# Expert gates spread in three passes over 40, 40 and 48 sub-tiles instead of four passes over 32

## What is computed

```python
q = (h @ wq).reshape(B, S, PEER_HEADS, 2, PEER_HALF)
sc = jnp.einsum('bshcd,cnd->bshcn', q, keys)
# top 16 of each half, then top 16 of the 256 sums, per token and head
expert = i1 * N_SUBKEYS + i2               # 128 * 128 experts
gate = jax.nn.softmax(best_v, axis=-1)
u = jnp.take(u_tab, ex, axis=0)
act = gelu(jnp.einsum('thkd,td->thk', u, hx)) * gx
vv = jnp.take(v_tab, ex, axis=0)
out = jnp.einsum('thk,thkd->td', act, vv)
```

## Time and profile before

| | |
|---|---|
| median of three runs | 2258.52 us |
| the profiled execution's time | 2252.36 us |
| its span | 2250.6 us |
| mean granted TensorE clock | 0.987 of full |
| TensorE matmuls | busy 2162.7 us, 21816 matmuls |
| VectorE | busy 1588.3 us |
| ScalarE | busy 1092.5 us |
| GpSimd | busy 336.4 us |

### The profile page before, as it was taken

One profiled execution on the slowest core, in us unless ns is written; L12 is line 12 of the kernel. 1 busy time (PEld: TensorE's weight loads), 2 busy tenths in 40 slices (PEclk: granted clock), 3 DMA queues, 4 the chain that ended last, 5 costly groups with the idle time before them and its releaser, 6 DMA issues.

```text
span 2250.6 us, 55219 instructions
## 1 busy us (share of the span) xinstructions
PE 2162.7 (96%) x21816; PEld 1939.7 (86%) x21816; DVE 1588.3 (71%) x3080; ACT 1092.5 (49%) x1881; POOL 336.4 (15%) x166
## 2 busy tenths in 40 slices
PE   8889999999999999999998899999999999999997
PEld 8878999988888888788788789999888888887885
DVE  6645896876666667975576458968766666679755
ACT  5534455444444444444454344554444444444443
POOL 0022696000000000000000237950000000000000
PEclk9999999999999999999999999999999999999999
DMA  6212344434444444445342134443344444444451
GB/s 255 94 41 102 143 171 174 142 131 168 167 164 165 164 165 165 149 168 187 134 149 93 41 125 142 181 167 135 131 168 168 168 168 168 166 153 150 167 200 70
DMA packets 46618, 335.04 MB, mean 149 GB/s; under 512 B 5168, under 2 KB 5296, under 8 KB 6320
## 3 DMA queue, kind: packets, MB, share of 16 engines
q1 hardware_dynamic: 46512, 333.61, 41.2%
HBM read 332.54 MB, written 1.05 MB: 148 GB/s over the span
## 4 chain that ended last, share of the span: by engine, by line
PE 80%; issue 6%; POOL 6%; DVE 5%; ACT 1%; DMA 1%; POOLq 0%; SPq 0%; DVEq 0%; ACTq 0%
PE PS L1647 32%; PE PS L1624 23%; PE PS L1309 8%; PE PS L1636 6%; POOL low L435 5%; PE PS L1325 3%; PE PS L1489 1%; DVE low L1083 1%; PE PS L1527 1%; PE PS L1538 1%; DVE hot L1153 1%; DVE hot L1149 1%; DMA ring<-in_w_slabs 1%; ACT high L459 0%; PE PS L1357 0%
## 5 line engine op out<-in xcount | busy, mean ns | idle before, releaser
L648 ACT CAST high<-ring 128x1024 fp32r<-128x1024 f32 x512 | 535.6, 1048 | 602.1 <-PE PS L1624 443.2
L1624 PE MATMUL PS<-hTh,high 128*128 128x256 f32 x2048 | 594.8, 290 | 13.0 <-ACT GA L652 11.0
L1624 PE MATMUL PS<-hTh,low 128*128 128x256 f32 x2048 | 578.4, 282 | 0.0
L1624 PE MATMUL PS<-hTl,high 128*128 128x256 f32 x2048 | 577.0, 282 | 0.0
L1083 DVE TENSOR_TENSOR low<-ring,high 128x1024 fp32r<-128x1024 f32 x432 | 514.8, 1217 | 0.8 <-ACT high L648 0.6
L1624 PEld LDWEIGHTS PS<-hTh,high 128*128 128x128 f32 x2048 | 387.1, 189 | 17.7 <-ACT GA L652 9.7
L1624 PEld LDWEIGHTS PS<-hTl,high 128*128 128x128 f32 x2048 | 387.6, 189 | 0.0
L1624 PEld LDWEIGHTS PS<-hTh,low 128*128 128x128 f32 x2048 | 387.3, 189 | 0.0
L1647 PE MATMUL PS<-high,WH 128*128 128x512 f32 x1024 | 323.6, 397 | 0.0
L1647 PE MATMUL PS<-low,WH 128*128 128x512 f32 x1024 | 317.9, 392 | 0.0
L1647 PE MATMUL PS<-high,WL 128*128 128x512 f32 x1024 | 316.4, 390 | 0.0
(11 more groups left out here) (251 smaller groups left out, 2980.1 us busy)
## 6 DMA issues: line engine op xcount, KB each, us to landing
ring<-in_peer_slabs SPq DMA_DIRECT2D x256, 1024.0 KB, 4.8
ring<-in_w_slabs SPq DMA_DIRECT2D x58, 1024.0 KB, 4.8
xres<-in_x SPq DMA_DIRECT2D x2, 512.0 KB, 4.3
out<-obuf SPq DMA_DIRECT2D x2, 512.0 KB, 2.6
cst<-in_consts SPq DMA_DIRECT2D x1, 680.0 KB, 10.1
praw<-in_p_t SPq DMA_DIRECT2D x1, 512.0 KB, 14.8
gfin<-in_g_final SPq DMA_DIRECT2D x1, 512.0 KB, 5.6
vec<-in_vecs SPq DMA_DIRECT2D x1, 356.0 KB, 7.0
```

The costliest lines, as they stand in the source:

```text
L648: act.copy(high[:, (c0[L] + j) % DEEP], ring[:, place, half * D:(half + 1) * D]).then_inc(part_hi, 1)
L1624: ins = mm(PS[:, 6 + j % 2, 0:SEQ], u[:, b, ks], h[:, k], start=n == 0, stop=n == 3 * KT - 1)
```

## The change

The 128 tiles are gated in three passes over tiles 0 to 39, 40 to 79 and 80 to 127 instead of four over 32. `GA` holds 80 tiles in place of 64, so the joint stretch has `JOINT` = 48 steps, of which the last 16 have no spread. Eight more tiles (`A_LOOP` = 48) are made in the first stretch, their `low` by GpSimd; the transposes come at tile 44. The second stretch is 32 tiles with one spread each. The late stretch is 32 steps of spread and spend, then 48 spends. A spread still has 24 matmuls, now of 40 or 48 columns; `hot2` and `is_i2` are laid out for 48, and the narrower passes use the first 40. `WH`, `WL`, `hot1`, `hot2`, `is_i2`, `decoded` and `repeats` are moved behind the larger `GA`. The host lays out the slabs of `peer_u` and `peer_v` to match.

```diff
-NQ = 4
-QT = NSUB // NQ
-HELD = 2 * QT
+STARTS, WIDTHS = (0, 40, 80), (40, 40, 48)
+NQ, WIDEST = len(WIDTHS), max(WIDTHS)
+HELD = WIDTHS[0] + WIDTHS[1]
+JOINT = NSUB - HELD
-A_FIRST, A_SECOND, A_TOP, A_LOOP = 16, 32, 36, 40
+A_FIRST, A_SECOND, A_TOP, A_LOOP = 16, 32, 44, 48
...
-        WH = place("WH", R + 16384, [2, SEQ], F32R)
+        WH = place("WH", R + 20480, [2, SEQ], F32R)
...
-        hot2 = place("hot2", R + 18432, [2, 3, GROUP, QT], BF16)
-        is_i2 = place("is_i2", R + 19200, [2, GROUP, QT], BF16)
+        hot2 = place("hot2", R + 22528, [2, 3, GROUP, WIDEST], BF16)
+        is_i2 = place("is_i2", R + 23680, [2, GROUP, WIDEST], BF16)
...
-                    dve.tensor_tensor(hot2[:, b].rearrange("p q t (a c) -> p q t a c", c=REP),
+                    dve.tensor_tensor(hot2[:, b, :, :, 0:width].rearrange("p q t (a c) -> p q t a c", c=REP),
...
-                    for g in spreads_after(e):
-                        first_chunk(g, g % 2, g == NGROUPS - 1)
+                    first_chunk(e - A_LOOP, e % 2, e == HELD - 1)
...
+                for s in range(NGROUPS, JOINT - 1):
+                    split_uv(s + 1, s % RING + 1)
+                    split_w(s + 1, s + 1, s + 1)
...
-                            ins = mm(PS[:, 4 + b, t * QT:(t + 1) * QT], hot1[:, b, t], hot2[:, b, part, t], start=part == 0, stop=part == 2)
+                            ins = mm(PS[:, 4 + b, t * width:(t + 1) * width], hot1[:, b, t], hot2[:, b, part, t, 0:width], start=part == 0, stop=part == 2)
...
-                with pe.Fori(0, HELD // 4) as i:
+                with pe.Fori(0, NGROUPS // 4) as i:
                     for j in range(4):
-                        spread(4 * i + (j + NGROUPS), j % 2)
+                        spread(4 * i + (j + NGROUPS), j % 2, 1)
                         hidden(4 * i + (j + HELD), j, 2 * j, second=True)
                         spend(4 * i + j, j, 2 * j + 1, low_dve, v0[L] + 2 + 2 * (4 * i + j))
-                with pe.Fori(HELD // 4, (HELD + QT) // 4) as i:
+                with pe.Fori(NGROUPS // 4, JOINT // 4) as i:
                     for j in range(4):
-                        spread(4 * i + (j + NGROUPS), j % 2)
-                        spend(4 * i + j, j, j, low_dve, v0[L] + (HELD + 1) + 4 * i + j)
+                        hidden(4 * i + (j + HELD), j, 2 * j, second=True)
+                        spend(4 * i + j, j, 2 * j + 1, low_dve, v0[L] + 2 + 2 * (4 * i + j))
```

More of the change, by code:

```diff
@@ L741, in _ @@
+                with act.Fori(0, NGROUPS // RING - 1) as i:
                     for j in range(RING):
[L742 to L749, removed]
+                        step(i, j, RING * i + j)
@@ L750, in _ @@
+                for s in range(NGROUPS - RING, JOINT - 2):
+                    step(s // RING, s % RING, s, s < NGROUPS)
+                for s in range(JOINT - 2, JOINT):
                     act.wait_ge(w_lo, NSUB * L + 1 + s)
[L751 to L754, removed]
+                    act.wait_ge(part_used, c0[L] + C_UV + 2 * s + 1)
@@ L755, in _ @@
                     gelu(s, s)
[L756 to L771, removed]
+                    split_w(s + 1, s + 1, s + 1, C_UV + 2 * s - 1)
@@ L772, in late @@
+                    for n in ((0,), (1, 2))[s - JOINT + 2]:
+                        split_vv(0, n)
+                def late(n, i, j, place, more=True, again=False):
+                    split_w(n, place, j + 1, C_VV - 1 + n)
                     if more:
@@ L774, in late @@
                     if again:
-                        repeat(n + (HELD + NGROUPS + 2), n + 2, j % 2)
-                with act.Fori(0, QT // 8 - 1) as i:
+                        repeat(n + (2 * NGROUPS + 2), n + 2, j % 2)
+                with act.Fori(0, NGROUPS // 8 - 1) as i:
                     for j in range(8):
[L779 to L782, removed]
+                        late(8 * i + j, i, j, 8 * i + (j + JOINT + 1), again=True)
+                for n in range(NGROUPS - 8, NGROUPS):
+                    if n == NGROUPS - 1:
+                        act.wait_ge(gated, NGROUPS * NQ * (L + 1))
+                    late(n, n // 8, n % 8, place_of(n + JOINT + 1), again=n < NGROUPS - 2)
+                with act.Fori(NGROUPS // 8, HELD // 8 - 1) as i:
                     for j in range(8):
-                        late(8 * i + j, i, j)
+                        late(8 * i + j, i, j, 8 * i + (j + JOINT + 1 - HELD))
                 for j in range(7):
-                    late(HELD - 8 + j, HELD // 8 - 1, j, j < 5)
+                    late(HELD - 8 + j, HELD // 8 - 1, j, place_of(HELD - 8 + j + JOINT + 1), j < 5)
                 for k in range(4):
@@ L1205, in step @@
                     split_w(s + 1, s + 1, j + 1)
[L1207 to L1223, removed]
+                dve.wait_ge(ga_ready, NSUB * L + STARTS[2])
+                with dve.Fori(0, NGROUPS // RING - 1) as i:
+                    for j in range(RING):
+                        step(RING * i + j, j, RING * i + j, 1)
@@ L1224, in _, with last_chunk @@
+                for s in range(NGROUPS - RING, NGROUPS):
+                    step(s, s % RING, s, 1, s == NGROUPS - 1)
+                for s in range(NGROUPS, JOINT - 1):
+                    split_uv(s + 1, s % RING + 1)
+                    split_w(s + 1, s + 1, s + 1)
+                split_vv(0, 0)
+                split_w(JOINT, JOINT, JOINT)
                 dve.wait_ge(ga_ready, NSUB * (L + 1))
-                def last_chunk(n, j, last=False):
+                def last_chunk(n, j, place, last=False):
@@ L1626, in hidden, with spread @@
                     ins.then_inc(part_used, 1)
-                def spread(g, b):
+                def spread(g, b, chunk):
+                    width = WIDTHS[chunk]
                     pe.wait_ge(hots_made, g0 + 1 + g)
@@ L1665, in _ @@
                 ins.then_inc(slot_ps, 1)
-                for e in range(A_TOP, A_LOOP + 4):
-                    hidden(e, e, e, by_dve=e >= POOL_U)
-                    if e in (A_LOOP, A_LOOP + 2):
-                        spread(e // 2 - A_LOOP // 2, e // 2 % 2)
-                with pe.Fori(0, (HELD - A_LOOP - 4) // 4) as i:
-                    for j in range(4):
-                        hidden(4 * i + (j + A_LOOP + 4), j, j, by_dve=True)
-                        spread(6 * i + (2 + 3 * j // 2), 3 * j // 2 % 2)
-                        if j % 2:
-                            spread(6 * i + (2 + 3 * j // 2 + 1), (3 * j // 2 + 1) % 2)
@@ L1678, in _ @@
-                with pe.Fori(0, HELD // 4) as i:
+                for e in range(A_TOP, A_LOOP):
+                    hidden(e, e, e)
+                for e in range(A_LOOP, A_LOOP + 4):
+                    hidden(e, e, e, by_dve=True)
+                    spread(e - A_LOOP, e % 2, 0)
+                with pe.Fori(1, NGROUPS // 4) as i:
+                    for j in range(4):
+                        hidden(4 * i + (j + A_LOOP), j, j, by_dve=True)
+                        spread(4 * i + j, j % 2, 0)
@@ L1691, in _ @@
+                with pe.Fori((JOINT + NGROUPS) // 4, NSUB // 4) as i:
+                    for j in range(4):
+                        spend(4 * i + j, j, j, low_dve, v0[L] + (JOINT + 1) + 4 * i + j)
                 for n in range(4):
```

86 lines of the change are left out of this document (40 added, 46 removed).

## The result

The changed kernel takes 2199.49 us (median of four runs, 2196.3 to 2205.14) against 2257.01 before (four runs): 0.9747 of the time, 95% interval 0.9724 to 0.977. That is 57.5 us less; forecast were 54.6 less and 2204 us.

The account below looks back on a forecast made before the run. TensorE was taken as the bound, busy 96% of the span. Layer gains 22.9 + 6.4 - 1.6 = 27.7 and 22.9 + 5.6 - 1.6 = 26.9, together 54.6 us, gave 2204 us, range 2195 to 2228.

Parts of the forecast that it names:

- Part 1: Joint stretch: 32 spreads a layer fewer, bare joint steps of 5.60 us; gain 22.9 us a layer.
- the late term: Third pass: VectorE's step taken as 3.52 us against TensorE's 3.47; 1.6 us lost a layer.
- Part 2: Spread matmuls of 40 or 48 columns: lower bound, taken, no added cost; upper bound 20.7 us over both layers.
- the line: Matmul time from the 256- and 512-column rows: 0.42 ns a column plus 10.6, giving 24.1 ns at 32 columns.
- Part 3: Second stretch: one tile per spread, 3.54 us steps, one 1.2 us stall at full clock; gain 6.4 and 5.6 us.
- Part 4: First stretch: eight more tiles, GpSimd's subtractions 2.36 us each under TensorE's 2.85, so no further cost.
- Part 5: Third pass: VectorE's step 3.48 to 3.56 us against TensorE's 3.47; 1.6 us lost a layer.
- Paid columns: Rival on TensorE's wider spreads: every column is paid, 20.7 us more, 2221 us; chance 0.24.
- VectorE's third pass: Rival: VectorE sets the third pass at 3.87 us a step, 22 us more, 2226 us; chance 0.08.
- Slow hot2: Rival: VectorE's hot2 falls to one element a cycle, 1.37 us not 0.75, 38 us more, 2242; chance 0.05.
- A second slot: Rival: TensorE matmuls above 32 columns take 50 ns for 25, 115 us more, 2319 us; chance 0.05.

Follow-up runs that it names:

- experiment 3: Changed kernel with 32 spreads a layer added again (24 constant-operand matmuls of 48 columns each, result unused): 2246.6 us, ratio 0.9956.
- experiment 1: Changed kernel with every spread matmul cut to 32 columns, VectorE's one-hots keeping their width: 2198.08 us, ratio 0.9744.
- experiment 2: Changed kernel with spreads of 64, 96 and 112 columns in the three passes: 2266.57 us, ratio 1.0046.
- experiment 8: Kernel before, four passes of 32, with only the buffers moved to the changed kernel's addresses: 2254.59 us, ratio 0.9991.
- experiment 5: Changed kernel with VectorE instead of GpSimd subtracting tiles 40 to 47: 2196.8 us, ratio 0.9738.
- experiment 4: Changed kernel with hot1 made by eight VectorE instructions instead of one in the third pass: 2230.15 us, ratio 0.9899.

## Why the prediction was right, step by step

**Part 1** held. It put 22.9 us a layer on the missing spreads; putting them back costs 22.6 where they stand and 22.9 to 23.1 in the whole expert part (experiment 3). It had the bare joint step at 5.60 us where it is 5.64, 0.6 us a layer too good, because the tile behind a spend takes 2.88 and not the 2.85 of tiles in a row. Measured with the late term, first spend to closing matmuls is 69.3 us shorter; less the 16 hidden tiles that moved ahead (45.6) that is 23.7 against 22.9 - 1.6 = 21.3 forecast.

**Part 2** held at its lower bound, and experiments 1 and 2 show why: 40 and 48 columns are still within the 25.8 ns that a matmul takes anyhow. The reason given then, that the 32-column row lies above the line, was thin: the line was drawn through f32 matmuls, and these don't have its 10.6 ns. Had the widths been 64, the spread would have cost 0.09 us more.

**Part 3** had the right mechanism and was 1.5 us a layer too good: gains of 4.9 and 4.0 us for 6.4 and 5.6. The stall came out at 1.09 us (forecast 1.2), with no fall of the clock. What was missing is, by its place, the turn of TensorE's loop: every fourth spread takes 0.75 instead of 0.62 to the next matmul, six times a layer, 0.8 us; the other steps are 3.55 and not 3.54, 0.4; and the last two spreads with the stall take 0.2 more. The chain of the changed kernel shows it as a tile of 3.08 us at each turn:

```profile
442.63 0.61 PE PS L1609 x24
443.25 3.08 PE PS L1596 x24
446.33 0.61 PE PS L1609 x24
```

That the old pattern's stalls went is read from the two traces; no run changes the order alone. In layer 0 the trace of before has four stalls of 0.57 us from start to start, then 2.24 and 0.85, and 2.2 on the slow tile, 7.6 in all; after has 1.3. The gain is less than the difference because more tiles stand behind a spread (2.93 us where the sum counts 2.85) and the loop turns come on top. The 0.8 us by which the slow tile differed between the layers isn't a matter of the layer: in experiment 8 the same stretch takes 97.73 us in layer 0 and 98.72 in layer 1, the other way round.

**Part 4** held: 22.8 us for eight tiles forecast, 133.17 - 110.35 = 22.8 measured (22.6 in layer 1), and GpSimd off the path (experiment 5). The transposes' move cost nothing.

**Part 5** had VectorE's step right (3.48 to 3.56; it is 3.48) and its price wrong: 1.6 us a layer forecast, none paid. Two things were off. TensorE's own step is 3.44, and VectorE starts the pass ahead of need, so that falling behind by 1.3 us reaches nobody. For experiment 4 I reckoned 2 us of lead (14.5 us a layer forecast); it is some 1.7 (14.7 and 14.8 paid), so the price of nothing here was near its edge. The prediction should have asked how far VectorE may lag, not only whose step is longer.

**The rivals.** Paid columns: excluded by experiment 1. VectorE's third pass: it isn't at 3.87 but at 3.48, and only with 0.5 us more does it set the time. Slow hot2: it takes 0.65 us at 40 columns and 0.76 at 48, about as reckoned, and not 1.37. A second slot: none up to 112 columns. The rows of hot2 after, by shape (columns as in the earlier trace rows):

```profile
L1131 DVE TENSOR_TENSOR hot<-is_i,repeats 128x960 bf16<-128x960 bf16 x128 | 83.4, 651 | 0.0
L1131 DVE TENSOR_TENSOR hot<-is_i,repeats 128x1152 bf16<-128x1152 bf16 x64 | 48.4, 757 | 0.0
```

**Sum.** 28.4 and 28.0 us a layer for 27.7 and 26.9. The near hit is in part luck: the second stretch was 3.1 us too good over both layers, the rest 4.8 too bad (2.4 a layer). By the runs the 56.4 us are 45.2 for the count (22.6 a layer, experiment 3), 8.9 for the second stretch and some 3 for the shorter steps below, to within 1 us.

**Left open.** The late step with a spread is 0.033 us shorter than before, and a joint one 0.013, which makes some 3 us of the 56. Neither the width (experiment 1) nor the addresses (experiment 8) do it. The matmuls put back in experiment 3 have the old step, the spreads beside them the new one. What differs was not found. One candidate no run tests: the results of the eight tokens of a spread stand 32 columns apart in PSUM in the kernel before and in experiment 8, and 40, 48 or 56 apart in the changed kernel and in experiments 1 and 2, which all have the shorter spend behind a spread; the added matmuls of experiment 3, all in one place, have the longer.

## What to carry to other kernels

A small matmul has a price per instruction; find the width up to which more columns ride along, then do the same work in fewer and wider matmuls. Before widening, count what the other engines do for each of them: here VectorE's step in the last pass became 0.04 us longer than TensorE's, and a full engine costs nothing as long as its lag stays within its lead. When a stretch gets a simple one-to-one order the stalls of its old pattern can go as well, here 9 of 56 us by the traces.

## What the runs showed of the chip

- The start-to-start time of a bfloat16 matmul with its own weight load is 25.6 to 25.9 ns at 32, 40 and 48 columns, 29.6 at 64, 42.3 at 96, 48.8 at 112. The fp32r matmuls take 118.5 ns at 256 columns and 226.7 at 512, 12 and 13 ns above their columns at 2.4 GHz.
- TensorE's granted clock stayed at 1.00 after a wait of 1.09 us behind two spreads, and after waits of 1.35 to 1.42 us between whole tiles in the first stretch. It was 0.61 over the next tile where waits of 0.52 and 1.42 us came with a single spread between them, and 0.52 where these were 2.10 and 0.64.
- In ScalarE's two loops over tiles 0 to 31, whose body has casts and `gelu`, each start of the body loaded the table twice, 1.28 us each, and held TensorE up by 1.5 us; written out, these loads went. It isn't every such loop: the one of the joint stretch has casts and `gelu` as well and shows no table load.
